# The first column blocks behind seven norms, computed from values that are not yet normalised

## The chip, the core and the metric

The kernel runs on one core of one Trainium2 chip. The core has TensorE (PE, matrix products), VectorE (DVE), ScalarE (ACT), GpSimd (POOL) and SyncE (SP, which issues nearly all DMAs). Each engine works through its own queue in order and waits on semaphores. The metric is device time in microseconds (us), the median of several runs.

## What is computed

A sequence of 256 positions with 1024 features passes through two blocks of two layers each, all in fp32 accuracy. With LN a LayerNorm and RMS an RMS norm:

```
x = LN(x; ln0)
for l in 0, 1:                                   # first block
    x = LN(a*x + mix(x @ w_in[l]) @ w_out[l]; ln1)      # attention, pooling, mLSTM
    u, g = split(x @ w_up[l])
    x = LN(a*x + (silu(conv3(g)) * u) @ w_down[l]; ln2)
for l in 0, 1:                                   # second block
    sh1, sc1, g1, sh2, sc2, g2 = split(silu(c) @ w_ada[l] + b_ada[l])
    h = RMS(x)*(1 + sc1) + sh1                   # rms0
    x = x + g1 * (conv and band attention of (h @ w_in2[l])) @ w_out2[l]
    h = RMS(x)*(1 + sc2) + sh2                   # rms1
    x = x + g2 * (dense SwiGLU (l = 0: ffn_gu, ffn_down) or 8 experts, top 2 (l = 1))(h)
```

## The kernel before

**Layout.** Activations stand transposed: 8 tiles of 128 features by 256 positions (`xT`, `hT`). Weights come in chunks of 1 MB (8 tiles of 128 rows by 256 columns: a column block) through a ring of four slots; SP issues a load when the slot's last reader is done.

**Split products.** For accuracy with fast products a weight is split: ACT copies a rounded high half (`whi`, L1027), DVE subtracts it for the low half (`wlo`, L1403). Activations are split likewise into `HH` (ACT, L1075) and `HL` (DVE, L1486). A product is then three matmuls (`mm3`), 48 for a column block (`pair`). There are buffers for two split chunks, so ACT and DVE work two chunks ahead (`two_ahead`, `ahead`), and the high half of chunk n+2 waits until PE has used chunk n.

**Norm.** `norm_tile` subtracts a pilot mean (DVE, L1436, LayerNorms only) and squares (ACT, L1051); in `norm_finish` PE sums over features with a matrix of ones, partial sums first and then the last two tiles. ACT and DVE make variance, root (L1060, L1063) and reciprocal (L1471), DVE centres (L1460) and multiplies (L1480), ACT applies weight and shift (L1070). While the statistics are made PE runs six filler products (`busy`, from constants). The first column block behind the norm is a `pair_whole`: the raw fp32 weights times `hT`, tile by tile as L1070 delivers them, 16 fp32 products of two records each. Meanwhile ACT makes all of `HH` and DVE then all of `HL` (`low_parts`). The second block is a `pair`. This goes for seven norms: ln0, ln1 (twice), ln2 of layer 0, rms0 (twice), rms1 of layer 0.

**Who uses the first block.** Behind ln0 and ln2 it is the query input `cq` (ACT L1079). Behind ln1 it is w_up's block 0: ACT taps it (L1237), DVE convolves (L1725), ACT applies SiLU (L1240; in layer 0 also to the row c, L1245), DVE gates (L1713) and makes the low part (`midl`, L1715). Behind rms0 ACT takes the sigmoid (L1274) and DVE the gate (L1809), then five taps of a convolution (L1782, L1786), then splits w_in2's third block. Behind rms1 it is ffn_gu's block 0.

**Modulation.** sh1 to g2 of both layers take 96 steps on DVE (`mod_step`, L1499), each with a 512 KB load into one of two buffers (SP, L1982). They are spread in three times 32: one behind each of w_up's blocks 1 to 21 of both layers and of ffn_gu's, and the other 11 between the chunks of w_down or ffn_down.

## Time and profile before

| | |
|---|---|
| median of 3 runs | 2084.1 us (2083.78 to 2084.38) |
| the profiled execution | 2083.09 us |
| its span, first to last instruction | 2081.1 us |
| busy: PE, DVE, ACT | 98%, 84%, 64% of the span |
| mean granted clock of PE | 0.995 |

Busy time of PE includes filler, and the ends of matmuls are modelled, so short waits between them are hidden in it. The experts of the last layer (from about 1066 us) are not touched by the change.

### The profile page before, as it was taken

The numbers are of one execution on the slowest core, as the hardware profiler recorded it, in microseconds if no ns is written. First come the engines' busy times: TensorE is split into PE (matmuls) and PEld (weight loads), VectorE is DVE, ScalarE is ACT, GpSimd is POOL, SyncE is SP. The second block draws the span as 40 slices with busy tenths as digits, with TensorE's granted clock in tenths as the row PEclk, the third lists the DMA queues.
The fourth block names the chain that finished last, engine by engine and source line by source line (L and its number), as shares of the span: only waits on it lengthen the run. The fifth ranks groups of instructions, "written<-read, shape, count | busy, mean of one in ns | idle before, by whom it ended". The sixth has DMA issues, their size and how long they took to land.

```text
span 2081.1 us, 31128 instructions
## 1 busy us (share of the span) xinstructions
PE 2038.9 (98%) x12718; PEld 1792.9 (86%) x12718; DVE 1754.4 (84%) x2299; ACT 1339.6 (64%) x1839; POOL 3.6 (0%) x23
## 2 busy tenths in 40 slices
PE   9999999999999999999989999999999999999998
PEld 8889999889998789998788888888888888888886
DVE  6779986789987967787869998888989889898987
ACT  4655545655545565445667777777777777777775
POOL 0000000000000000000000000000000000000000
PEclk9999999999999999999999999999999999999999
DMA  5358783348784438785449999999999999999994
GB/s 209 127 196 280 256 299 135 128 185 287 252 302 176 162 112 306 273 301 202 144 165 358 364 362 348 345 363 366 362 351 344 362 365 361 347 351 367 364 359 183
DMA packets 94179, 578.53 MB, mean 278 GB/s; under 512 B 11600, under 2 KB 14672, under 8 KB 35792
## 3 DMA queue, kind: packets, MB, share of 16 engines
q1 hardware_dynamic: 92592, 570.03, 74.0%
q10 hardware_dynamic: 1152, 3.32, 0.4%
q0 software_dynamic: 288, 3.15, 0.4%
q8 instruction: 102, 1.67, 0.3%
q14 instruction: 45, 0.37, 0.0%
HBM read 572.27 MB, written 1.05 MB: 275 GB/s over the span
## 4 chain that ended last, share of the span: by engine, by line
PE 76%; DVE 17%; ACT 5%; DMA 1%; issue 1%; SPq 0%; DVEq 0%; ACTq 0%
PE bank L2061 46%; PE bank L512 28%; DVE wlo L1403 6%; DVE side L1499 2%; DVE arena L1725 2%; DMA ring<-in_w_in 1%; PE bank L2119 1%; ACT arena L1240 1%; DVE RSTD L1471 1%; DVE midl L1715 1%; ACT whi L1027 1%; ACT midh L1229 1%; DVE XC L1480 0%; DVE XC L1460 0%; ACT HH L1082 0%
## 5 line engine op out<-in xcount | busy, mean ns | idle before, releaser
L1027 ACT ACTIVATE whi<-ring 128x1024 fp32r<-128x1024 f32 (+1 forms) x766 | 756.0, 1020 | 148.7 <-PE bank L512 66.1
L1403 DVE TENSOR_TENSOR wlo_moe<-ring,whi 128x1024 fp32r<-128x1024 f32 x448 | 526.4, 1220 | 9.6 <-ACT whi L1027 6.9
L512 PE MATMUL bank<-HH,whi 128*128 128x256 f32 x1536 | 430.6, 280 | 4.3 <-DVE wlo L1403 3.0
L512 PE MATMUL bank<-HL,whi 128*128 128x256 f32 x1536 | 424.3, 276 | 0.0
L512 PE MATMUL bank<-HH,wlo 128*128 128x256 f32 x1536 | 424.3, 276 | 0.0
L1403 DVE TENSOR_TENSOR wlo<-ring,whi 128x1024 fp32r<-128x1024 f32 (+3 forms) x318 | 343.6, 1114 | 76.4 <-ACT whi L1027 76.2
L512 PEld LDWEIGHTS bank<-HH,whi 128*128 128x128 f32 x1536 | 288.4, 188 | 8.7 <-DVE wlo L1403 4.2
L512 PEld LDWEIGHTS bank<-HL,whi 128*128 128x128 f32 x1536 | 288.5, 188 | 0.9 <-issue 0.5
L512 PEld LDWEIGHTS bank<-HH,wlo 128*128 128x128 f32 x1536 | 288.4, 188 | 0.0
L1403 DVE TENSOR_TENSOR extra_lo<-ring,extra_hi 128x1024 fp32r<-128x1024 f32 x224 | 264.4, 1221 | 14.7 <-ACT extra_hi L1027 14.4
L1027 ACT ACTIVATE extra_hi<-ring 128x1024 fp32r<-128x1024 f32 x224 | 229.8, 1061 | 41.1 <-PE bank L2061 41.1
L2061 PE MATMUL bank<-whi,xg 128*128 128x512 f32 x672 | 220.5, 396 | 0.0
L512 PE MATMUL bank<-midh,whi 128*128 128x256 f32 x528 | 148.3, 281 | 5.7 <-DVE midl L1715 3.3
L2061 PEld LDWEIGHTS bank<-whi,xg 128*128 128x128 f32 x672 | 126.3, 188 | 27.1
L512 PE MATMUL bank<-midl,whi 128*128 128x256 f32 x528 | 147.3, 279 | 0.0
L512 PE MATMUL bank<-midh,wlo 128*128 128x256 f32 x528 | 147.2, 279 | 0.0
L2061 PE MATMUL bank<-whi,xg_hh 128*128 128x512 f32 x336 | 134.7, 401 | 0.3 <-DVE wlo_moe L1403 0.3
L2061 PE MATMUL bank<-whi,xg_ht 128*128 128x512 f32 x336 | 131.6, 392 | 0.0
L2061 PE MATMUL bank<-wlo_moe,xg 128*128 128x512 f32 x336 | 131.6, 392 | 0.0
L2061 PE MATMUL bank<-wlo_moe,xg_hh 128*128 128x512 f32 x336 | 131.5, 391 | 0.0
L1499 DVE CUSTOM_DVE_ANT_0 side<-side,vec 128x1024 f32<-128x1024 f32 x96 | 122.8, 1279 | 0.5 <-DMA side<-in_w_ada 0.5
L512 PEld LDWEIGHTS bank<-midh,whi 128*128 128x128 f32 x528 | 100.7, 191 | 6.9 <-DVE midl L1715 3.7
(293 smaller groups left out, 3463.5 us busy)
## 6 DMA issues: line engine op xcount, KB each, us to landing
ring<-in_moe_gate SPq DMA_DIRECT2D x112, 1024.0 KB, 5.8
ring<-in_moe_up SPq DMA_DIRECT2D x112, 1024.0 KB, 6.7
ring<-in_moe_down SPq DMA_DIRECT2D x112, 1024.0 KB, 5.5
side<-in_w_ada SPq DMA_DIRECT2D x96, 512.0 KB, 4.3
ring<-in_w_up SPq DMA_DIRECT2D x44, 1024.0 KB, 4.9
ring<-in_w_in SPq DMA_DIRECT2D x32, 1024.0 KB, 5.5
ring<-in_w_down SPq DMA_DIRECT2D x32, 704.0 KB, 5.2
ring<-in_ffn_gu SPq DMA_DIRECT2D x22, 1024.0 KB, 4.8
```

Of the source, the lines that this page charges most:

```text
L512: return pe.matmul(out, lhsT, rhs, start=start, stop=stop, skip_group_check=True)
L1027: a.activation(hi, part, ACT.Copy).then_inc(*made.up(("hi", n, i)))
L1229: a.activation(MIDH[:, j, :], GC[j % 3], ACT.Copy).then_inc(*a_ffn.up(("mid", *key, j)))
L1240: a.activation(gc, gc, ACT.Silu).then_inc(*a_ffn.up(("silu", "w_down", l, j)))
L1403: v.tensor_tensor(lo, part, hi.bitcast(F32), ALU.subtract).then_inc(*done.up(("lo", n, i)))
L1471: v.reciprocal(RSTD[:, 0, :], RSTD[:, 0, :]).then_inc(*v_norm.up((s.name, "rstd")))
L1499: v.tensor_tensor_reduce(side_in[n % 2], side_in[n % 2], crow, 1.0, W(f"b_ada{l}", at), ALU.mult, ALU.add, modT[:, l, at:at + 1]).then_inc ...
L1715: v.tensor_tensor(MIDL[:, j, :], gc, MIDH[:, j, :].bitcast(F32), ALU.subtract).then_inc(*v_ffn.up(("mid", *key, j)))
L1725: v.scalar_tensor_tensor(gc[:, s:S], b[:, S:512 - s], W(f"w_fconv{l}", (2 - s) * NJ + j), gc[:, s:S], ALU.mult, ALU.add).then_inc(*v_ffn.u ...
L2061: return pe.matmul(out, lhsT, rhs, start=start, stop=stop, skip_group_check=True)
L2119: tm = pe.transpose(b[:, 128 * k:128 * k + 128], SGB[n % 2][:, 128 * k:128 * k + 128], ident)
```

## The change

Seven norms no longer have a filler and a `pair_whole`. While the tiles arrive, ACT makes a scaled copy of each, `ZT` (the tile times the norm's weight, not centred and not divided), with the weight (and for LayerNorms the shift) as extra columns. PE multiplies the first block's raw weights with `ZT` (`ahead_pair`): one of the eight pairs of products stands between the sums of the last tiles, three in rms0 of layer 0, none in ln0, the rest behind the sums. When the statistics are in, DVE scales the result, adds the product of mean and extra column (`ahead_made`), and the readers add the other extra column as a bias. `HH` and `HL` are now made in turn with the normalised tiles, and the second block takes them as they come (`pair_as_made`). Centring waits until the tile's copy in `ZT` is made. The 96 modulation steps are placed anew (`MOD_AT`): 24 in each layer of the first block (behind every second block of w_up, and 13 in w_down), 48 in the dense feed-forward (32 in ffn_gu, 16 in ffn_down); their loads follow six chunks behind the step two before (`mod_loads`).

The core of the diff; the reference to the same pattern in other stages is left out:

```diff
+        at_z = (2 * NJ + 3) * S
+        ZT = arena[:, at_z:at_z + 8 * (S + 2)].rearrange("p (k c) -> p k c", k=8)
+        AH, ends_ah = SQ[:, 6:8, :], small[:, 16:20]
...
+        AHEAD = {"ln0": ("w_in", 0, 1), ("ln2", 0): ("w_in", 1, 1), ("rms1", 0): ("ffn_gu", 0)}
+        for l in range(DEPTH):
+            AHEAD |= {("ln1", l): ("w_up", l, 0), ("rms0", l): ("w_in2", l, 0)}
+
+        MOD_AT = {}
+        for l in range(DEPTH):
+            MOD_AT |= {("w_up", l, j): 1 for j in range(1, NJ, 2)} | {("w_down", l, m, c): 1 for m in range(7) for c in range(2)}
+            del MOD_AT["w_down", l, 6, 1]
+        MOD_AT |= {("ffn_gu", j): 2 if j % 2 else 1 for j in range(1, NJ)}
+        MOD_AT |= {("ffn_down", m, c): 1 for m in range(8) for c in range(2)}
+        mod_slots = [CH[key] for key in sorted(MOD_AT, key=lambda key: CH[key]) for _ in range(MOD_AT[key])]
+        assert len(mod_slots) == 96, len(mod_slots)
+        mod_loads = {}
+        for n in range(2, 96):
+            mod_loads.setdefault(mod_slots[n - 2] + 6, []).append(n)
...
+            def ahead_pair(s):
+
+                key = AHEAD[s.name]
+                n = CH[key]
+                order = FIRST_ORDER if s.name == "ln0" else tuple(range(8))
+                cols_ = S + 2 if s.about else S + 1
+                banks = [take(*key, m, until=[(v_norm, s.name, "scaled", m)]) for m in range(2)]
+                w = raw_tile(n)
+                pe.wait_ge(*ARRIVED[n])
+                for k in order:
+                    pe.wait_ge(*a_norm(s.name, "z", k))
+                    for m in range(2):
+                        tm = mm(banks[m][:, 0:cols_], w[:, k, 128 * m:128 * m + 128], ZT[:, k, 0:cols_], k == order[0],
+                                k == order[-1])
+                    if k == order[-1]:
+                        tm.then_inc(*p_w.up(("raw", n), (*key, 0), (*key, 1)))
+                    yield
+
...
+                first = ahead_pair(s) if s.name in AHEAD else None
+                between = (1, 3, 5) if s.direct == 8 else (lim,) if s.direct == 2 else ()
...
                 for k in tiles:
...
+                    if first and k in between:
+                        next(first)
                 pause()
                 pause()
-                if end:
+                if first:
+                    for _ in first:
+                        pass
+                elif end:
                     busy(end, s.name)
...
+            def pair_as_made(key, src, until):
+
+                n = CH[key]
+                b = take(*key, until=until)
+                ws = [half(n, m) for m in range(2)]
+                for k in range(8):
+                    pe.wait_ge(*ready_h(src, k))
+                    for m in range(2):
+                        tm = mm3(b[:, S * m:S * m + S], [x[:, k, :] for x in ws[m]], H(k), k + m == 0, k == 7)
+                tm.then_inc(*p_w.up(("half", n, 0), ("half", n, 1), (*key, 0), (*key, 1)))
...
-                pair_whole(("w_in", l, 1), [(a_proj, "cqs0", l)])
-                pair(("w_in", l, 2), src, [(a_proj, "xp1", l)])
+                pair_as_made(("w_in", l, 2), src, [(a_proj, "xp1", l)])
...
+                    if j > 0:
+                        (pair_as_made if j == 1 else pair)(("w_up", l, j), ("ln1", l), [(v_ffn, "gated", "w_down", l, j)])
...
+                if s.name in AHEAD and s.name != "ln0":
+                    ahead_tile(s, k)
+
...
+            def ahead_tile(s, k):
+
+                gain, *_ = ends = ahead_columns(s)
+                if k == (FIRST_ORDER[0] if s.name == "ln0" else 0):
+                    for i, x in enumerate(ends if s.about else ends[1:]):
+                        a.activation(ZT[:, :, S + i], x, ACT.Copy).then_inc(*a_norm.up((s.name, "column", i)))
+                a.wait_ge(*(v_norm(s.name, "xc", k) if s.about else s.ready(k)))
+                a.activation(ZT[:, k, 0:S], (XC if s.about else s.src)[:, k, :], ACT.Copy, scale=gain[:, k:k + 1]).then_inc(
+                    *a_norm.up((s.name, "z", k)))
+
...
                     a.activation(RS[:, 0, :], PS[BANK[s.name, "mean"]][:, 0:S], ACT.Square, scale=1.0 / s.kt).then_inc(*a_norm.up((s.name, "mean2")))
+                    for k in beside:
+                        ahead_tile(s, k)
                     a.wait_ge(*v_norm(s.name, "var"))
...
-                if not then:
-                    for k in range(0, 8, 2):
-                        a.wait_ge(*a_norm(s.name, "dst", k + 1))
-                        a.activation(HH[:, k:k + 2, :], dst[:, k:k + 2, :], ACT.Copy).then_inc(
-                            *a_norm.up((s.name, "hh", k), (s.name, "hh", k + 1)))
+                    if behind:
+                        ahead_tile(behind, k)
+                    if not then and k % 2:
+                        a.wait_ge(*a_norm(s.name, "dst", k))
+                        a.activation(HH[:, k - 1:k + 1, :], dst[:, k - 1:k + 1, :], ACT.Copy).then_inc(
+                            *a_norm.up((s.name, "hh", k - 1), (s.name, "hh", k)))
...
-            norm_dev(N["ln0"])
+            for k in FIRST_ORDER[0:2]:
+                ahead_tile(N["ln0"], k)
+            norm_dev(N["ln0"], FIRST_ORDER[2:3])
+            for k in FIRST_ORDER[3:]:
+                ahead_tile(N["ln0"], k)
             split(CH["w_in", 0, 2], (0,))
             affine(N["ln0"], hT, lambda k: W("ln0_g", k), lambda k: W("ln0_b", k))
             split(CH["w_in", 0, 2], (1,))
...
                 split(CH["w_in", l, 3])
+                for m in range(2):
+                    a.wait_ge(*v_norm(IN[l], "ahead", m))
+                    a.activation(cq[:, m, :], AH[:, m, :], ACT.Identity, bias=ends_ah[:, 2 * m + 1:2 * m + 2]).then_inc(
+                        *a_proj.up(("cq0", l)))
+                    a.activation(SQ[:, m, :], AH[:, m, :], ACT.Square, bias=ends_ah[:, 2 * m + 1:2 * m + 2]).then_inc(
+                        *a_proj.up(("cqs0", l)))
...
+                    if j == 0:
+                        a.wait_ge(*v_norm(("ln1", l), "ahead", 1))
+                        a.activation(AH[:, 1, :], AH[:, 1, :], ACT.Identity, bias=ends_ah[:, 3:4]).then_inc(*a_ffn.up(("first", l)))
+                        a.wait_ge(*a_ffn("first", l))
+                        gate_in = AH[:, 1, :]
+                    else:
+                        a.wait_ge(*p_w("w_up", l, j, 1))
+                        gate_in = PS[BANK["w_up", l, j]][:, S:512]
+                    a.activation(gc, gate_in, ACT.Identity, bias=W(f"b_fconv{l}", j),
                                  scale=W(f"w_fconv{l}", 2 * NJ + j)).then_inc(*a_ffn.up(("tap", l, j)))
                     a.wait_ge(*v_ffn("conv", l, j))
...
+                    if c == 0:
+                        a.wait_ge(*v_norm(("rms0", l), "ahead", 1))
+                        a.activation(SG[:, 0, :], AH[:, 1, :], ACT.Sigmoid, bias=ends_ah[:, 3:4]).then_inc(*a_att.up(("sg", l, c)))
+                        return
...
+                    if j == 0:
+                        a.wait_ge(*v_norm(("rms1", 0), "ahead", 1))
+                        a.activation(GC[0], AH[:, 1, :], ACT.Silu, bias=ends_ah[:, 3:4]).then_inc(
...
                     v.wait_ge(*p_norm(s.name, "mean"))
+                    if s.name in AHEAD:
+                        for k in range(lo, hi):
+                            v.wait_ge(*a_norm(s.name, "z", k))
                     v.scalar_tensor_tensor(XC[:, lo:hi, :], bc(PS[BANK[s.name, "mean"]][:, 0:S], 2), -1.0 / s.kt, XC[:, lo:hi, :], ALU.mult,
...
+                    if s.name in AHEAD and j > 0:
+                        low_part(s, 2 * j - 2)
+                if s.name in AHEAD:
+                    low_part(s, 6)
+
+            def low_part(s, k):
+                v.wait_ge(*a_norm(s.name, "hh", k + 1))
+                v.tensor_tensor(HL[:, k:k + 2, :], hT[:, k:k + 2, :], HH[:, k:k + 2, :].bitcast(F32), ALU.subtract).then_inc(
+                    *v_norm.up((s.name, "hl", k), (s.name, "hl", k + 1)))
...
+            def ahead_made(s):
+
+                key = AHEAD[s.name]
+                if s.about:
+                    v.wait_ge(*v_norm(s.name, "rstd"))
+                    v.scalar_tensor_tensor(RS[:, 1, :], PS[BANK[s.name, "mean"]][:, 0:S], -1.0 / s.kt, RSTD[:, 0, :], ALU.mult,
+                                           ALU.mult).then_inc(*v_norm.up((s.name, "nmr")))
+                v.wait_ge(*p_w(*key, 1))
+                lo, n = (0, 2) if s.about else (1, 1)
+                for m in range(2):
+                    v.tensor_copy(ends_ah[:, 2 * m + lo:2 * m + 2], PS[BANK[(*key, m)]][:, S:S + n]).then_inc(
+                        *v_norm.up((s.name, "ends", m)))
+                for m in range(2):
+                    v.tensor_tensor(AH[:, m, :], PS[BANK[(*key, m)]][:, 0:S], RSTD[:, 0, :], ALU.mult).then_inc(
+                        *v_norm.up((s.name, "scaled", m), *([] if s.about else [(s.name, "ahead", m)])))
+                if s.about:
+                    for m in range(2):
+                        v.wait_ge(*v_norm(s.name, "scaled", m))
+                        v.scalar_tensor_tensor(AH[:, m, :], RS[:, 1, :], ends_ah[:, 2 * m:2 * m + 1], AH[:, m, :], ALU.mult,
+                                               ALU.add).then_inc(*v_norm.up((s.name, "ahead", m)))
...
+            def mod_beside(*key):
+                for _ in range(MOD_AT.get(key, 0)):
+                    mod_step(next(mod_steps))
...
             norm_finish(N["ln0"])
-            split(CH["w_in", 0, 2], (0,))
-            low_parts(N["ln0"])
-            split(CH["w_in", 0, 2], (1,))
+            split(CH["w_in", 0, 2])

             for l in range(DEPTH):
                 split(CH["w_in", l, 3])
+                ahead_made(N[IN[l]])
...
                     two_ahead(CH["w_up", l, j])
-                    gc, b = GC[j % 3], PS[BANK["w_up", l, j]]
+                    gc = GC[j % 3]
+                    if j == 0:
+                        ahead_made(N["ln1", l])
+                    gate_in = AH[:, 1, :] if j == 0 else PS[BANK["w_up", l, j]][:, S:512]
                     v.wait_ge(*a_ffn("tap", l, j))
...
-                    if j > 0:
-                        mod_step(l, j - 1)
+                    mod_beside("w_up", l, j)
...
                 def gate(c):
                     ahead(CH["w_in2", l, c])
-                    v.wait_ge(*a_att("sg", l, c))
-                    v.tensor_tensor(Z[:, c, :], PS[BANK["w_in2", l, c]][:, 0:S], SG[:, c % 2, :], ALU.mult).then_inc(
-                        *v_att.up(("z", l, c)))
+                    if c == 0:
+                        ahead_made(N["rms0", l])
+                        v.wait_ge(*a_att("sg", l, c))
+                        v.scalar_tensor_tensor(Z[:, c, :], AH[:, 0, :], ends_ah[:, 1:2], SG[:, 0, :], ALU.add, ALU.mult).then_inc(
+                            *v_att.up(("z", l, c)))
...
+                modulated_gain(1, l)
...
-                rms_modulated(1, l)
+                norm_finish(N["rms1", l])
...
+                    if j == 0:
+                        ahead_made(N["rms1", 0])
                     if j > 0:
                         gated(("ffn_down",), ("ffn_gu", j - 1), j - 1)
-                    if j > 0:
-                        mod_step(2, j - 1)
+                    mod_beside("ffn_gu", j)
...
+                g.wait_ge(*p_w("raw", CH["w_in", l, 1]))
...
+                g.wait_ge(*p_w("raw", CH["w_in2", l, 0]))
...
+            def mod_load(n):
+                if n >= 2:
+                    sp.wait_ge(*v_mod("step", n - 2))
+                sp.dma_start(side_in[n % 2], t["w_ada"][n // 48, n // 8 % 6, n % 8]).then_inc(s_side[n % 2], 16)
...
-                    next(mod)
+                    mod_load(0)
+                    mod_load(1)
...
+                for k in mod_loads.get(n, ()):
+                    mod_load(k)
```

## Rows read from the trace of the kernel before

**Rows 1.** The page, busy time by engine, and shares of the chain that ended last.
```profile
PE 2038.9 (98%) x12718; PEld 1792.9 (86%) x12718; DVE 1754.4 (84%) x2299; ACT 1339.6 (64%) x1839; POOL 3.6 (0%) x23
...
PE 76%; DVE 17%; ACT 5%; DMA 1%; issue 1%; SPq 0%; DVEq 0%; ACTq 0%
```

**Rows 2.** Windows (stretch, length, busy by engine with count, granted clock, DMA share, GB/s).
```profile
160.00:245.00 85.00, 85.00 (x753) 85.00 (x752) 77.20 (x122) 47.05 (x76) 0.00 (x0) 1.00 0.82 277
247.00:280.40 33.40, 30.37 (x243) 29.59 (x242) 29.18 (x49) 15.28 (x26) 0.00 (x0) 0.95 0.76 254
270.22:273.63 3.41, 3.41 (x19) 3.41 (x18) 3.41 (x6) 0.53 (x2) 0.00 (x0) 0.50 0.59 207
...
569.00:592.00 23.00, 20.37 (x159) 19.71 (x158) 19.73 (x33) 9.63 (x16) 0.00 (x0) 0.93 0.78 267
...
785.00:885.00 100.00, 100.00 (x884) 100.00 (x884) 79.08 (x111) 49.54 (x75) 0.00 (x0) 1.00 0.78 283
```

**Rows 3.** Timeline of PE, two waits (start, length, instruction, idle time before and releaser).
```profile
268.34 0.38 PE L512 MATMUL bank<-midh,whi 128*128 128x256 f32 x1 [1.61 <-DVE midl L1715]
...
749.89 0.38 PE L512 MATMUL bank<-HH,whi 128*128 128x256 f32 x1 [1.10 <-DVE wlo L1403]
```

**Rows 4.** Timeline of DVE, one round in w_up of layer 0.
```profile
199.57 1.28 DVE L1499 CUSTOM_DVE_ANT_0 side<-side,vec 128x1024 f32<-128x1024 f32 x1
...
203.04 0.99 DVE L1725 SCALAR_TENSOR_TENSOR arena<-bank,vec,arena 128x255 f32<-128x255 f32 x2
...
205.19 1.28 DVE L1499 CUSTOM_DVE_ANT_0 side<-side,vec 128x1024 f32<-128x1024 f32 x1
```

**Rows 5.** Timeline of PE behind the sums: ln0, ln1, rms0 of layer 0.
```profile
18.76 7.14 PE L512 MATMUL bank<-hT,ring 128*128 128x256 f32 x32 [2.30 <-ACT hT L1070]
...
132.51 2.75 PE L512 MATMUL bank<-cst 128*128 128x256 f32 x12
136.74 7.14 PE L512 MATMUL bank<-hT,ring 128*128 128x256 f32 x32 [1.48 <-ACT hT L1070]
...
646.25 3.69 PE L512 MATMUL bank<-SQ,cst 128*128 128x256 f32 x16 [0.33 <-DVE SQ L1439]
```

**Rows 6.** DMA issues: the modulation's loads (count, size, us to landing).
```profile
side<-in_w_ada SPq DMA_DIRECT2D x96, 512.0 KB, 4.3
```

**Rows 7.** Timeline of ACT behind ln1 of layer 0.
```profile
136.00 1.09 ACT L1070 ACTIVATE hT<-XC,vec 128x256 f32<-128x256 f32 x2 [2.28 <-DVE XC L1480]
...
141.32 2.17 ACT L1075 ACTIVATE HH<-hT 128x512 fp32r<-128x512 f32 x4
...
148.10 1.04 ACT L1245 ACTIVATE side<-side 128x1024 f32<-128x1024 f32 x1
```

**Rows 8.** Timeline of ACT, squares and splits in w_out and w_out2.
```profile
113.67 0.75 ACT L1051 ACTIVATE SQ<-XC 128x256 f32<-128x256 f32 x2 [3.09 <-DVE XC L1436]
114.32 1.99 ACT L1027 ACTIVATE whi<-ring 128x1024 fp32r<-128x1024 f32 x2
...
746.62 0.94 ACT L1051 ACTIVATE SQ<-xT 128x256 f32<-128x256 f32 x2 [3.10 <-DVE xT L1763]
```

**Rows 9.** Timeline of DVE behind ln1 of layer 0.
```profile
133.75 1.75 DVE L1471 RECIPROCAL RSTD<-RSTD 128x256 f32<-128x256 f32 x1
...
136.93 0.69 DVE L1480 TENSOR_TENSOR XC<-XC,RSTD 128x512 f32<-128x512 f32 x1
...
141.96 2.50 DVE L1486 TENSOR_TENSOR HL<-hT,HH 128x512 fp32r<-128x512 f32 x4 [1.68 <-ACT HH L1075]
```

**Rows 10.** Timeline of DVE behind ln0.
```profile
14.97 1.75 DVE L1471 RECIPROCAL RSTD<-RSTD 128x256 f32<-128x256 f32 x1
...
25.68 1.23 DVE L1403 TENSOR_TENSOR wlo<-ring,whi 128x1024 fp32r<-128x1024 f32 x1
```

**Rows 11.** Timeline of DVE behind rms0 of layer 0.
```profile
661.14 0.42 DVE L1809 TENSOR_TENSOR arena<-bank,RS 128x256 f32<-128x256 f32 x1 [0.96 <-ACT RS L1274]
...
664.01 2.35 DVE L1403 TENSOR_TENSOR wlo<-ring,whi 128x1024 fp32r<-128x1024 f32 x2
```

More of the change, by code:

```diff
@@ L840, in pe_program @@
                 for j in range(NJ):
-                    if j == 0:
-                        pair_whole(("w_up", l, 0), [(v_ffn, "gated", "w_down", l, 0)])
-                    else:
-                        pair(("w_up", l, j), ("ln1", l), [(v_ffn, "gated", "w_down", l, j)])
+                    if j > 0:
+                        (pair_as_made if j == 1 else pair)(("w_up", l, j), ("ln1", l), [(v_ffn, "gated", "w_down", l, j)])
                 for m in range(8):
@@ L1064, in norm_dev, with affine @@
                         *a_norm.up((s.name, "dev")))
-            def affine(s, dst, gain, bias, then=False):
+            def affine(s, dst, gain, bias, then=False, behind=None):
                 a.wait_ge(s_vec, 16)
@@ L1255, in act_program @@
                 else:
-                    affine(N["ln2", 1], xT, lambda k: W("ln2_g1", k), lambda k: W("ln2_b1", k), then=True)
+                    affine(N["ln2", 1], xT, lambda k: W("ln2_g1", k), lambda k: W("ln2_b1", k), then=True, behind=N["rms0", 0])
             def rms_modulated(which, l):
@@ L1501, in mod_step, with modulated_gain @@
                     *v_mod.up(("step", n), *([("mod", l, i)] if k == 7 else [])))
+            def mod_beside(*key):
+                for _ in range(MOD_AT.get(key, 0)):
+                    mod_step(next(mod_steps))
+            def modulated_gain(which, l):
+                sc = 8 if which == 0 else 32
+                v.wait_ge(*v_mod("mod", l, 1 if which == 0 else 4))
+                v.wait_ge(s_vec, 16)
+                v.scalar_tensor_tensor(amod[:, which, :], modT[:, l, sc:sc + 8], 1.0,
+                                       W("nmix%d" % l if which == 0 else "nffn%d" % l, 0, 8), ALU.add, ALU.mult).then_inc(
+                    *v_norm.up(((("rms0", "rms1")[which], l), "amod")))
             def low_of_mix(k, src, name):
@@ L1766, in dve_program @@
             for l in range(DEPTH):
[L1767 removed]
+                norm_finish(N["rms0", l])
+                v.wait_ge(*p_w("raw", CH["w_in2", l, 0]))
                 v.reduce_sum(rows32, ident.rearrange("p (r j) -> p j r", r=4), AX_X).then_inc(*v_tap.up(("rows32", l)))
@@ L2028, in sp_program @@
                         delayed_rows(l, 3)
-                for _ in range(steps_behind(chunks[n - NSLOT][0]) if NSLOT <= n < first_moe else 0):
-                    next(mod)
+                for k in mod_loads.get(n, ()):
+                    mod_load(k)
         def in_use(used):
```

114 lines of the change are left out of this document (39 added, 75 removed).

## The prediction

> **What bounds the kernel now.** I read the page first, then the stretches by engine (windows), then the timelines around each norm. The page shows TensorE (PE) busy almost all the time, and the chain that ended last runs through PE for three quarters of the span and through VectorE (DVE) for most of the rest [rows 1]. So only time that PE loses in waits, or spends on filler, can be won. The windows show two kinds of stage [rows 2]. In a steady feed-forward stretch PE starts 753 matmuls in 85 us, 0.113 us each: a split column block (48 matmuls) takes 5.44 us and no wait is seen. At the two passages from w_up to w_down, 243 matmuls take 33.4 us where 27.5 would do, and 159 take 23.0 where 18.0 would do; about 0.2 us of each difference is the pilot product. The waits there are for DVE [rows 3]. The reason is in DVE's own round: one modulation step of 1.2 us, two low parts, convolution and gating, and the next step starts 5.62 us after this one [rows 4]. That is 0.18 us per column block more than PE's 5.44, so DVE falls back until PE has nothing to do.
>
> The second loss is the norm itself. After the sums of ln1 PE runs 12 filler records (2.75 us), idles 1.48 us and computes the first column block from fp32 values, 32 records in 7.14 us, 0.44 us for each of 16 products [rows 5]. The second block starts at 143.5 and ends at 149.0, 16.5 us after the fillers began.
>
> **What the change removes: the fall-back of DVE.** In w_up every second block keeps its modulation step. DVE's round becomes 5.62 - 1.2/2 = 5.02 us on average against PE's 5.44. The waits at both passages go: 5.9 - 0.2 = 5.7 and 5.0 - 0.2 = 4.8, together **-10.5 us**. The steps that leave go mostly to the dense feed-forward stage, where DVE is busy 79 of 100 us and half a step more per block (0.6 us of 5.44) fits [rows 2]. Each moved step takes its 512 KB load along: SyncE waits for step n-2 before it issues load n, and the next weight load stands behind that wait. A step's load lands in 4.3 us [rows 6] and the weights are fetched four chunks ahead, so I cost it at nothing; without that cover, one late load would stall DVE by at most those 4.3 us. GpSimd's fills now wait for the early block instead of the last low part, which is sooner: nothing.
>
> **What it adds at a norm.** Eight scaled tiles (z) on ScalarE (ACT); no row shows a Copy with a column scale, so I bound it: 0.33 us (spacing of the plain squares) and 0.50 (spacing of the affine tiles, which have scale and bias) [rows 7, 8]; I take 0.43, nearer the second because it too reads a column. On DVE, for a LayerNorm: one product of mean and deviation, two tiny copies, two scalings, two additions; from 0.34 to 0.42 us each and 0.1 for a copy, about 2.05 us; for an RMS norm 1.1 us. On ACT one extra pass before the first tap, 0.55 us as an affine tile. The extra columns add 2 of 256 to 16 products, under 0.1 us.
>
> **ln1, step by step (twice).** DVE's chain after the sums: reciprocal to 135.5, tiles 2 and 3 normalised from 136.93 [rows 9]. With a low part (2.50/4 = 0.63) behind each pair, a pair costs 0.71 + 0.61 + 0.63 = 1.94 us. ACT keeps up: two affine tiles 1.09 and one copy 0.54 are 1.66 with the waits between [rows 7]. The last low part ends at about 144.3, the second block, made as the low parts come, at 144.3 + 12 x 0.113 = 145.7 instead of 149.0. That is 3.3 us gained, if the third and fourth blocks are there.
>
> They are not. The wait for the scaled block stands in ACT's queue ahead of the split of w_up 3. DVE: two low parts of w_up 2 to 147.0, the new pieces to 149.0. ACT: added pass and tap to 150.1. DVE: convolution 0.99 [rows 4] to 151.2. ACT: SiLU 0.42, in layer 0 also the row c (0.95 [rows 7]), then the high half 1.04; DVE its low half 1.22: ready at 155.0 in layer 0 and 154.1 in layer 1. PE wants it at 145.7 + 5.44 = 151.1 and waits 3.9 and 3.0 us. Before, it started there at 143.5 + 5.5 + 5.44 = 154.5. So the 3.3 us are lost again, with 0.5 on top in layer 0 and -0.4 in layer 1; DVE then delivers w_up 4 another 0.4 late.
>
> And the sums come later. The split of w_out 2 starts on ACT right behind the squares of tiles 0 and 1 [rows 8]; now two columns (0.2) and two z stand before it, +1.1 us, and two more z before the next split, +0.45. DVE's residuals follow these splits, so the last tile is 1.6 us late. Sum: +0.5 + 0.4 + 1.6 = **+2.5 us** in layer 0, -0.4 + 0.4 + 1.6 = **+1.6** in layer 1.
>
> **ln0.** The centring of tiles 0 and 1 now waits for their z. These are the second and third ACT jobs behind the square root, so the reciprocal that began at 14.97 begins 1.9 us later, at 16.9. From reciprocal to last low part takes 144.3 - 133.75 = 10.6 us as in ln1: 27.5. Only then come both low halves of the second block (2.36): 29.8, and PE wants both before its first product. Before, it began at 18.76 + 6.9 = 25.6 and the second half, ready at 26.9, was in time [rows 5, 10]. **+4.2 us**; PE idles some 8 us in it, as its early block is over by 22.
>
> **ln2 of layer 0.** Same chain: -3.3, the sums 0.8 later (one pair of products stands among them), and the split of chunk 4 stands on ACT behind four copies of the scaled block, about +1.4: **-1.1 us**.
>
> **rms0 (twice).** Here the wait has a short path. The third block's low part follows the first gate and five taps on DVE: gate at 661.14, low part at 664.01, done 1.22 later [rows 11]; sums had ended at 649.9 [rows 5], so it began 14.1 behind them. Now the gate waits for the new pieces: last low part at 10.3, 1.1 for the pieces, 0.5 for the sigmoid, gate and taps 2.9, so low part from 15.0 to 16.3. The second block is over at 11.8; PE idles 4.5 us, then starts the third block 0.4 us later than before (15.9). In layer 0, three pairs of products (0.86 each) stand among the sixteen records of the sums [rows 5], where 0.33 us were idle: +2.4: **+2.8 us**. In layer 1 two modulation steps now lie on DVE in the last row of ffn_down, before the last residual: about +1.0, **+1.4 us**.
>
> **rms1 of layer 0.** The only clean one: no convolution between block and split. Second block over at 11.8 instead of 15.9 behind the sums; w_up 3's counterpart is ready at 16.7, wanted at 17.3. -4.1. But the split of w_out2 2, for which PE waits already (1.10 us [rows 3]), stands behind two squares [rows 8] and now also two z: +0.9. **-3.2 us**.
>
> **Clock.** With the fillers gone, the long waits matter for PE's clock. In the trace a wait of 1.61 us to 268.3 [rows 3], with shorter ones beside it, went ahead of a fall: from 270.2 the granted clock was 0.50, the 1.2 GHz level, for 3.4 us with 19 matmuls where 30 fit: 11 x 0.113 = 1.2 us lost, up to 1.7 if all of it is used [rows 2]. The 1.48 us idle behind ln1's fillers left the clock at full. The new waits are 8, 3.9, 3.0, 4.5 and 4.5 us; I take five falls at 1.06 us after what they hide: **+5.3 us**. Bounds: none, and 1.7 for each of six (w_out2's wait too), 10.2.
>
> The Trainium skill (TensorE: Matmul & The Clock Gate, "HAM oscillation — how this bites in real kernels") says that waits between bursts of matmuls let the clock fall to half, again at every such wait. By that rule all of the new waits are paid in full and the sum is that of the third rival below; the trace agrees as far as it goes, with its fall at 270.2.
>
> **Sum.** -10.5 + 2.5 + 1.6 + 4.2 - 1.1 + 2.8 + 1.4 - 3.2 = -2.3; with the clock +3.0. The profiled execution took 2083.1 us (span 2081.1); the median of the runs, 2084.1, lies 1.0 above, so I predict **2087.1 us**: no difference to speak of. Within 0.2% (4.2 us) a measurement of this kernel does not tell a change from none.
>
> **Rivals.** (1) The waits behind the norms go for good, because the work between block and third split is shorter than I add up: -10.5 - 3.3 x 3 - 4.1 x 3 = -33 at most, 2051 us. For it speaks that PE's filler and idle time is real [rows 5]; against it the order of ACT's and DVE's programs, which is fixed. Chance 0.06. (2) The same waits, but the clock holds and z costs 0.33: -2.3 - 2.5 = -5, 2079 us, just faster. For it: the waits of 1.5 us that cost no clock. Chance 0.14. (3) Slower: each new wait is followed by a full fall, -2.3 + 10.2 = +7.9, 2092 us. It decides from 6.5 us of falls on. For it: the fall behind a wait of 1.61 us. Chance 0.33. (4) The moved steps do not free w_up, as DVE, starting each w_up late, never catches up: +3.0 + 10.5, 2098 us. Against it: 0.42 us per block over 17 blocks. Chance 0.05. My forecast, a draw within 0.2%, has 0.42.
>
> **Range.** From just past rival 2 to past rival 3: 2077 to 2096; the likeliest case alone, 2080 to 2088. Faster 0.20, same 0.42, slower 0.38.
>
> **What the next profile would show.** No PE wait for a low part of w_down or of midl at the two passages; modulation steps two apart in w_up. PE idle before the fourth w_up block, released by the low part, 3 to 4 us; before the third w_in2 block about 4.5 us; before the second block of ln0 about 8 us, followed by stretches at 0.50. Scaled tiles of 0.33 to 0.50 us on ACT. If PE goes from the fourth block on without a wait, the ACT queue is not what I think, and I am wrong to the fast side; if waits at the passages remain, to the slow side.

## The result and the profile after

The changed kernel took 2114.8 us (median of 4, 2112.2 to 2116.8) against 2083.9 before: a ratio of 1.0146, 95% interval 1.0131 to 1.0161. That is 31 us slower, where 3 were forecast and at most 12 allowed for. The profiled execution took 2114.85 us (span 2111.4).

Three lines of the page after: PE's and DVE's busy time, the chain that ended last by engine, and the group of the modulation steps (busy, mean ns, then DVE's idle time ahead of them and what ended it).

```profile
PE 2039.8 (97%) x12634; PEld 1788.3 (85%) x12634; DVE 1766.3 (84%) x2339; ACT 1362.9 (65%) x1912; POOL 3.5 (0%) x23
...
PE 59%; DVE 24%; ACT 9%; DMA 6%; issue 2%; DVEq 0%; SPq 0%; ACTq 0%
...
L1608 DVE CUSTOM_DVE_ANT_0 side<-side,vec 128x1024 f32<-128x1024 f32 x96 | 122.7, 1281 | 17.1 <-DMA side<-in_w_ada 16.4
```

The last of these in the kernel before:

```profile
L1499 DVE CUSTOM_DVE_ANT_0 side<-side,vec 128x1024 f32<-128x1024 f32 x96 | 122.8, 1279 | 0.5 <-DMA side<-in_w_ada 0.5
```

Against [rows 1], PE's share of the chain falls from 76 to 59% and the shares of DVE, ACT and DMA grow: the work that ended last now runs through PE's suppliers. DMA, at 1% before, has 6, and the third line says which loads DVE waits for: it stood still 16.4 us for those of modulation steps. Before, that was 0.5 us.

Windows of the changed kernel (columns as in [rows 2]): behind ln0, the two passages, and two stretches of the dense feed-forward stage.

```profile
24.40:34.30 9.90, 4.73 (x22) 4.76 (x23) 8.04 (x14) 5.70 (x10) 0.00 (x0) 0.50 0.38 122
266.30:282.50 16.20, 15.50 (x135) 15.30 (x134) 13.78 (x23) 8.14 (x13) 0.00 (x0) 1.00 0.67 233
576.20:592.40 16.20, 15.55 (x135) 15.34 (x134) 13.78 (x23) 8.16 (x15) 0.00 (x0) 1.00 0.67 230
800.00:900.00 100.00, 94.84 (x813) 93.07 (x812) 82.41 (x119) 43.40 (x68) 0.00 (x0) 1.00 0.86 300
903.00:968.00 65.00, 61.09 (x516) 59.18 (x515) 52.16 (x81) 26.70 (x47) 0.00 (x0) 1.00 0.91 318
```

The passages are nearly cleared: 135 matmuls in 16.2 us, at full clock. One large loss is in the fourth row: 813 matmuls in 100 us where the kernel before had 884 [rows 2], 71 x 0.113 = 8 us lost in this stretch alone, in a stage in which nothing was lost before.

PE's long waits in the changed kernel, from its timeline (last in brackets: the idle time and what ended it).

```profile
29.57 0.55 PE L530 MATMUL bank<-HH,whi 128*128 128x256 f32 x1 [8.86 <-DVE wlo L1486]
...
162.58 0.36 PE L530 MATMUL bank<-HH,whi 128*128 128x256 f32 x1 [3.40 <-DVE wlo L1486]
...
472.54 0.36 PE L530 MATMUL bank<-HH,whi 128*128 128x256 f32 x1 [2.47 <-DVE wlo L1486]
...
671.69 0.39 PE L530 MATMUL bank<-HH,whi 128*128 128x256 f32 x1 [4.11 <-DVE wlo L1486]
...
758.36 0.58 PE L530 MATMUL bank<-HH,whi 128*128 128x256 f32 x1 [2.14 <-DVE wlo L1486]
...
912.15 0.39 PE L530 MATMUL bank<-midh,whi 128*128 128x256 f32 x1 [2.07 <-DVE midl L1839]
...
976.55 0.80 PE L530 MATMUL bank<-SQ,cst 128*128 128x256 f32 x1 [5.78 <-ACT SQ L1088]
...
994.03 0.55 PE L530 MATMUL bank<-HH,whi 128*128 128x256 f32 x1 [3.51 <-DVE wlo L1486]
```

Six are the waits of the prediction in their places: ln0, fourth block behind each ln1, third block behind each rms0, third block of w_out2. Two were not foreseen: 2.07 us at the passage from ffn_gu to ffn_down, for the same low part as at w_up's passages before, and 5.78 us ahead of the last sums of rms0 of layer 1.

To see where the 31 us lie, I read the same instruction in several timelines: the start of the first or last product of a stage. First column: the kernel before, us; then how much later each of three kernels is there (the two single parts are experiments, below).

| start of | before | changed | steps alone | early blocks alone |
|---|---|---|---|---|
| second block behind ln0 | 25.55 | +4.0 | +1.6 | +4.0 |
| w_out, layer 0 | 112.75 | +6.2 | +1.7 | +6.2 |
| last of w_up, layer 0 | 258.22 | +8.0 | +1.3 | +11.1 |
| last of w_down, layer 0 | 324.10 | +6.9 | -1.5 | +12.3 |
| w_out, layer 1 | 424.75 | +5.1 | -0.9 | +10.8 |
| last of w_up, layer 1 | 569.90 | +6.2 | -0.9 | +15.1 |
| last of w_down, layer 1 | 635.28 | +3.1 | -4.3 | +14.6 |
| last of w_in2's first blocks, layer 0 | 698.81 | +7.5 | -4.3 | +18.9 |
| last of w_out2, layer 0 | 760.83 | +10.0 | -4.4 | +19.6 |
| last of ffn_gu | 887.96 | +14.1 | +0.9 | +16.0 |
| last of ffn_down | 947.80 | +20.9 | +6.0 | +16.9 |
| second block behind rms0, layer 1 | 960.19 | +24.5 | +12.2 | +12.7 |
| last of w_in2's first blocks, layer 1 | 998.66 | +29.8 | +12.2 | +19.3 |

The +1.6 of the steps alone in the first row is not theirs, as nothing is changed there. Behind the same wait of 2.30 us the whole products of ln0 took 7.14 us at full clock in the kernel before [rows 5], but in this execution 8.83, with a stretch at the half clock:

```profile
18.70 8.83 PE L533 MATMUL bank<-hT,ring 128*128 128x256 f32 x32 [2.30 <-ACT hT L1154]
```

```profile
19.10:22.50 3.40, 3.40 (x10) 2.69 (x9) 3.33 (x5) 3.05 (x7) 0.00 (x0) 0.50 0.54 222
```

So a difference of 1.6 us between two single profiles is no sign of the change there.

### The profile page after: what moved, and what is told of

It reads as the page before. It is cut to its first block, busy times and chain, and to the rows that moved or that the text cites. A ratio compares the mean times of both kernels' runs of the same rounds, so it can differ in the third digit from the quotient of the medians.

```text
span 2111.4 us, 31090 instructions
## 1 busy us (share of the span) xinstructions
PE 2039.8 (97%) x12634; PEld 1788.3 (85%) x12634; DVE 1766.3 (84%) x2339; ACT 1362.9 (65%) x1912; POOL 3.5 (0%) x23
## 4 chain that ended last, share of the span: by engine, by line
PE 59%; DVE 24%; ACT 9%; DMA 6%; issue 2%; DVEq 0%; SPq 0%; ACTq 0%
PE bank L2173 45%; PE bank L530 12%; DVE wlo L1486 10%; DMA side<-in_w_ada 5%; DVE side L1608 4%; ACT whi L1064 3%; DVE arena L1852 2%; PE bank L2231 1%; ACT hT L1131 1%; DVE RSTD L1557 1%; ACT arena L1314 1%; DVE midl L1839 1%; DVE XC L1566 1%; DVE XC L1546 1%; ACT HH L1137 0%
## 5 line engine op out<-in xcount | busy, mean ns | idle before, releaser
L530 PE MATMUL bank<-HH,whi 128*128 128x256 f32 x1536 | 437.1, 285 | 37.1 <-DVE wlo L1486 32.6
L1608 DVE CUSTOM_DVE_ANT_0 side<-side,vec 128x1024 f32<-128x1024 f32 x96 | 122.7, 1281 | 17.1 <-DMA side<-in_w_ada 16.4
```

Of the source, the lines that this page charges most:

```text
L530: return pe.matmul(out, lhsT, rhs, start=start, stop=stop, skip_group_check=True)
L1608: v.tensor_tensor_reduce(side_in[n % 2], side_in[n % 2], crow, 1.0, W(f"b_ada{l}", at), ALU.mult, ALU.add, modT[:, l, at:at + 1]).then_inc ...
```

## The experiments

**First four: the two halves of the change.**

Steps alone (`mod_alone`): no early blocks, so all seven norms keep filler and whole products. The line that empties the list, in the changed kernel; the rest of the edit, left out here, brings back what a norm outside the list needs.

```diff
+        SEVEN = set(AHEAD)
+        AHEAD = {k: x for k, x in AHEAD.items() if k in ()}
```

> The kernel before with the new places of the modulation steps and of their loads alone; the seven norms keep filler and whole products. Theory A (the moved steps come back as waits for their loads: between the start of the dense feed-forward stage and the second block behind rms0 of layer 1 the changed kernel lost 24.5 - 5.3 = 19.2 us against the kernel before): the two passages give some 8.6 us, the dense stage takes some 19, so 2083.9 - 8.6 + 19.2 = about 2094 us. Theory B (the prediction's: moved steps cost nothing, the loss of 31 us is made at the norms): 2083.9 - 10.5 = about 2073 us.

Measured: 2096.6 us, ratio 1.0057 (1.0040 to 1.0073). The moved steps alone cost 11.6 us against the 2085.0 of the kernel before beside them; A holds, B falls. DVE's idle time until a step's load landed (us, times), from the view of the steps' tile:

```profile
  DMA side<-in_w_ada: 18.8, 23
```

Early blocks alone (`ahead_alone`): a step behind every block again, loads as before.

```diff
-            MOD_AT |= {("w_up", l, j): 1 for j in range(1, NJ, 2)} | {("w_down", l, m, c): 1 for m in range(7) for c in range(2)}
+            MOD_AT |= {("w_up", l, j): 1 for j in range(1, NJ)} | {("w_down", l, m, c): 1 for m in range(6) for c in range(2)}
...
-        MOD_AT |= {("ffn_gu", j): 2 if j % 2 else 1 for j in range(1, NJ)}
+        MOD_AT |= {("ffn_gu", j): 1 for j in range(1, NJ)}
...
-            mod_loads.setdefault(mod_slots[n - 2] + 6, []).append(n)
+            mod_loads.setdefault(mod_slots[n - 2] + 5, []).append(n)
```

> The changed kernel with the modulation steps where they were (a step behind every block of w_up and ffn_gu, 32 in each third), so only the early first blocks remain of the change. Theory A: 2114.8 - 10.6 = about 2104 us, no waits for modulation loads in the dense stage, the waits at the two passages from w_up to w_down back. Theory B: 2114.8 + 10.5 = about 2125 us.

Measured: 2103.2 us, 1.0089 (1.0072 to 1.0105), 18.2 us above before, as A has it. The two halves add up: 11.6 + 18.2 = 29.8, of the 31 measured together.

Loads sooner (`loads_sooner`): of the diff above only the last pair of lines, in the changed kernel.

> The changed kernel with one number changed: the load of step n is issued behind the fifth weight chunk after the block of step n - 2 and not behind the sixth. Theory A1 (the loads are late because SyncE issues them a block too late): most of the 19 us in the dense stage come back, about 2100 us. Theory A2 (with two buffers and three steps in two blocks the landing time itself, 5.9 us in that stage, is too long whatever the place of the issue): under 6 us come back, 2109 to 2115 us. Theory B (loads play no part): 2114.8 us.

Measured: 2108.5 us, 1.0114 (1.0095 to 1.0133): 6.4 us come back, just past what A2 allows and far from A1: the place of the issue is worth at most a third of the 19 us. The same line of the steps' tile for the changed kernel:

```profile
  DMA side<-in_w_ada: 16.4, 19
```

And for this kernel; two thirds of it stay:

```profile
  DMA side<-in_w_ada: 10.8, 11
```

Why it stays is seen in the changed kernel's dense stage, first in DVE's timeline, then in SyncE's.

```profile
845.99 1.28 DVE L1608 CUSTOM_DVE_ANT_0 side<-side,vec 128x1024 f32<-128x1024 f32 x1 [0.82 <-DMA side<-in_w_ada]
...
850.71 1.28 DVE L1608 CUSTOM_DVE_ANT_0 side<-side,vec 128x1024 f32<-128x1024 f32 x1
...
852.26 1.29 DVE L1608 CUSTOM_DVE_ANT_0 side<-side,vec 128x1024 f32<-128x1024 f32 x1 [0.26 <-DMA side<-in_w_ada]
...
858.48 1.28 DVE L1608 CUSTOM_DVE_ANT_0 side<-side,vec 128x1024 f32<-128x1024 f32 x1 [1.41 <-DMA side<-in_w_ada]
```

```profile
847.31 0.33 SPq L2106 DMA_DIRECT2D side<-in_w_ada  x1
849.58 0.33 SPq L2130 DMA_DIRECT2D ring<-in_ffn_gu  x1
852.03 0.33 SPq L2106 DMA_DIRECT2D side<-in_w_ada  x1
```

The step at 858.48 uses the buffer of the step at 850.71, two before it, which ends at 851.99. SyncE issues the load at 852.03, at once; it lands 6.4 us later, 7.7 after that step's start. In a rhythm of two steps in one block and one in the next, the three steps come due some 5.4, 9.7 and 6.6 us after the start of the one two before them (5.44 for a block, 1.2 for a step). Two of three are late, though the issue waits for nothing but the buffer. The chain that ended last, in the changed kernel from 790 to 860 us, goes from step to load to step; its shares by line there:

```profile
by line: DMA side<-in_w_ada 43.1%; DVE side L1608 22.9%; DVE wlo L1486 22.7%; ACT midh L1441 4.3%; DVE midl L1839 4.3%; DVE arena L1837 2.9%; issue 0.7%; DVE arena L1834 0.6%; DVE modT L1608 0.2%
```

Steps spread (`spread_alone`): as steps alone, but a step behind three of four blocks of w_up and one behind each block of the dense stage; loads five chunks behind, as in loads sooner.

```diff
+            MOD_AT |= {("w_up", l, j): 1 for j in range(1, NJ) if j % 4} | {("w_down", l, m, c): 1 for m in range(7) for c in range(2)}
...
+        MOD_AT |= {("ffn_gu", j): 1 for j in range(1, NJ)}
         MOD_AT |= {("ffn_down", m, c): 1 for m in range(8) for c in range(2)}
+        MOD_AT["ffn_gu", 11] = 2
```

> The kernel before with other places for the modulation steps: three of four blocks in w_up, 13 of 16 in w_down, one behind each block of the dense stage (one block has two); loads behind the fifth chunk. Theory A: the passages from w_up to w_down go as in the changed kernel and nothing comes back, 2083.9 - 8.6 = about 2075 us; DVE's round in w_up is then 5.62 - 1.2/4 = 5.32 us against PE's 5.44. If only the halving of the steps frees w_up, the passages keep part of their waits, 2079 us or more.

Measured: 2081.8 us, 0.9986 (0.9976 to 0.9995): 3.2 us won, not 9. ffn_gu runs without loss, but here too PE waits ahead of the last sums of rms0 of layer 1, as in its timeline:

```profile
947.70 0.80 PE L534 MATMUL bank<-SQ,cst 128*128 128x256 f32 x1 [5.57 <-ACT SQ L1112]
```

Between the last product of ffn_down and the second block behind rms0, 12.4 us before, lie 18.4 us. The steps in the last two rows of ffn_down wait for their loads and stand ahead of the last residual.

**Second four: places that cost nothing, and the order of the splits.**

Steps spread, last rows clear (`spread_clear`); this is the base of all later runs but one.

```diff
+            MOD_AT |= {("w_up", l, j): 1 for j in range(1, NJ) if j % 5} | {("w_down", l, m, c): 1 for m in range(7) for c in range(2)}
...
+        MOD_AT |= {("ffn_gu", j): 2 if j in (6, 11, 16) else 1 for j in range(1, NJ)}
+        MOD_AT |= {("ffn_down", m, c): 1 for m in range(6) for c in range(2)}
```

> The kernel before with the modulation steps spread once more: four of five blocks in w_up, 13 of 16 in w_down, one behind each block of ffn_gu (three blocks have two), and none in the last two rows of ffn_down, where the run with all 16 filled lost 6.0 us to late loads ahead of the last residual and half a clock window behind it. Theory: steps cost time only where their load comes late ahead of work that PE waits for, so this gains the passages (some 8 us) and loses about 1 us at each of the three double steps: about 2079 us against 2084 to 2085. If the last rows were not the cause, it stays at spread_alone's time, 2082 us.

Measured: 2077.4 us, 0.9962 (0.9949 to 0.9976), 7.7 us below before. The same line of the steps' tile, and the window of ffn_gu:

```profile
  DMA side<-in_w_ada: 0.2, 1
```

```profile
767.00:881.20 114.20, 114.20 (x1009) 114.17 (x1008) 92.00 (x129) 56.62 (x84) 0.00 (x0) 1.00 0.79 293
```

DVE waits for loads no more, and PE starts 1009 products in 114.2 us, 0.113 each. The moved steps pay when each load has time.

Two early blocks (`clean_two`): on this base, early first blocks behind ln2 of layer 0 and rms1 of layer 0 only.

```diff
+        AHEAD = {k: x for k, x in AHEAD.items() if k in (('ln2', 0), ('rms1', 0))}
```

> The last kernel with the early first block at two norms alone, ln2 of layer 0 and rms1 of layer 0. Theory (order of the queues: these two have no convolution or gate between the early block and the third block's split): 1.0 + 2.9 = 3.9 us below spread_clear, about 2075 us. Rival (any early block costs, as it takes the filler away and lets the clock fall): no better than spread_clear, 2079 us or more.

Measured: 2075.2 us, 0.9952 (0.9938 to 0.9965), 2.2 us below `spread_clear` where 3.9 were expected. So an early block can pay, but something takes a part.

Splits sooner (`splits_sooner`): in the changed kernel. The first part below is ACT's, the second DVE's (which leaves out j == 1 as well), the third is in the gate of both.

```diff
-                    two_ahead(CH["w_up", l, j])
+                    if j != 1:
+                        two_ahead(CH["w_up", l, j])
+                    if j == 0:
+                        two_ahead(CH["w_up", l, 1])
...
                         ahead_made(N["ln1", l])
+                        two_ahead(CH["w_up", l, 1])
...
-                    ahead(CH["w_in2", l, c])
+                    if c != 2:
+                        ahead(CH["w_in2", l, c if c == 3 else c + 1])
```

> The changed kernel with the splits of the next blocks moved ahead of the early block's own work: behind ln1 the split of w_up 3 stands ahead of ACT's wait for the scaled block and ahead of the convolution on DVE; behind rms0 the splits of the third and fourth blocks stand ahead of the gate. Theory (PE waits 3.7, 2.8, 4.4 and 3.8 us behind these four norms because the low part stands behind the block's own work): some 2 us come back at each ln1 and 3 to 5 at each rms0, 10 to 14 in all, 2101 to 2105 us. Rival (the waits only move on to the next block): 2112 to 2115 us.

Measured: 2110.1 us, 1.0117 (1.0102 to 1.0133): 4.7 us come back, not 10 to 14. The waits of 3.40 us at 162.58 and 4.11 at 671.69 are gone, but:

```profile
166.54 0.36 PE L530 MATMUL bank<-HH,whi 128*128 128x256 f32 x1 [1.64 <-DVE wlo L1490]
...
679.92 0.67 PE L530 MATMUL bank<-whi,HH 128*128 128x512 f32 x1 [1.99 <-DVE wlo L1490]
```

The waits are shorter and one block further on: the rival holds for more than half of what was hoped for.

All that was thought good (`six_sooner`): steps as in `spread_clear`, six early blocks (not ln0), splits sooner.

> The steps placed as in spread_clear, the early first block at six norms (ln0 keeps filler and whole products), and the splits sooner. If both theories hold, with 2 us less at each ln1 and 2 at each rms0 than without early blocks: about 2079 - 3.9 - 8 = 2067 us. If the clock's falls decide, 2079 us or more.

Measured: 2089.5 us, 1.0021 (1.0012 to 1.0031), 12 us above `spread_clear`. My theory of the order of the splits falls as a remedy: what DVE owes behind ln1 comes due later, at the passage to w_down, where four steps in five blocks leave it 5.62 - 1.2/5 = 5.38 us a round against PE's 5.44, no room to catch up:

```profile
270.48 0.39 PE L533 MATMUL bank<-midh,whi 128*128 128x256 f32 x1 [1.65 <-DVE midl L1888]
```

**Last four: single norms.**

Scaled tiles later (`clean_two_late`): as `clean_two`, but ACT makes each scaled tile behind the next splits (the False tells `norm_tile` to leave it out).

```diff
+                    if ("ln2", l) in AHEAD:
+                        for k in (0, 1) if m == 2 else (m - 1,) if m > 2 else ():
+                            ahead_tile(N["ln2", l], k)
                     for k in () if m == 0 else (0, 1) if m == 1 else (m,):
-                        norm_tile(N["ln2", l], k)
+                        norm_tile(N["ln2", l], k, False)
...
+                    if ("rms1", l) in AHEAD and c > 0:
+                        for k in (2 * c - 2, 2 * c - 1):
+                            ahead_tile(N["rms1", l], k)
                     for k in (2 * c, 2 * c + 1):
-                        norm_tile(N["rms1", l], k)
+                        norm_tile(N["rms1", l], k, c == 3)
```

> The kernel with steps spread and early blocks behind ln2 of layer 0 and rms1 of layer 0, with each scaled tile moved on ACT behind the next splits of w_down and of w_out2 instead of ahead of them. Theory (the scaled tiles delay the splits: 0.5 us in each of four rows of w_down, together 2.0 us; 0.9 us and a fall of the clock at the third block of w_out2, together 2.3): 2075.2 - 4.3 = about 2071 us. Rival (the tiles are not what delays them, or moved they delay the sums): 2075 us or more.

Measured: 2071.0 us, 0.9931 (0.9918 to 0.9945): as expected, and 13.5 us below the kernel before. In ACT's timeline of `clean_two` the scaled tile (L1132) stands ahead of the split (L1087):

```profile
739.63 0.49 ACT L1132 ACTIVATE arena<-xT,amod 128x256 f32<-128x256 f32 x1
740.03 1.99 ACT L1087 ACTIVATE whi<-ring 128x1024 fp32r<-128x1024 f32 x2
```

In `clean_two_late` the split follows the squares at once:

```profile
738.00 0.94 ACT L1111 ACTIVATE SQ<-xT 128x256 f32<-128x256 f32 x2 [3.05 <-DVE xT L1930]
738.84 1.99 ACT L1087 ACTIVATE whi<-ring 128x1024 fp32r<-128x1024 f32 x2
...
740.84 0.89 ACT L1132 ACTIVATE arena<-xT,amod 128x256 f32<-128x256 f32 x2
```

PE's wait for that block goes from 1.79 us in `clean_two`, with a stretch at the half clock behind it, to 1.11 in `clean_two_late`, at full clock, as before (1.10, [rows 3]):

```profile
742.46 0.38 PE L533 MATMUL bank<-HH,whi 128*128 128x256 f32 x1 [1.79 <-DVE wlo L1520]
```

```profile
741.27 0.39 PE L533 MATMUL bank<-HH,whi 128*128 128x256 f32 x1 [1.11 <-DVE wlo L1528]
```

The 396 products of w_down take 45.0 us again (47.0 in `clean_two`).

ln0 alone, and ln0 with the wait filled (`ln0_alone`, `ln0_filled`), on the base of `spread_clear`:

```diff
                 src = IN[l]
+                if src == "ln0":
+                    busy(18, "wait")
```

> The steps spread as in spread_clear (2077.4 us) and the early first block behind ln0 alone. From the changed kernel's trace: the second block starts 4.0 us later, and 10 us at the half clock follow the wait of 9.2 us; 2077.4 + 4.0 to 6.3 = 2081 to 2084 us. The prediction's term was +4.2 without the clock.

> The last kernel with 18 filler products (about 0.46 us each, 8.3 us) on TensorE in the wait behind the early block of ln0. If the half clock behind that wait costs time of its own, about 2 us come back against ln0_alone (second block at +4.0, nothing lost behind it); if it lies in time that is lost anyway, the time is that of ln0_alone.

Measured: 2081.7 us (median of 11, 2079.9 to 2086.1) and 2080.7 (11, 2077.7 to 2082.0), each against 2084.5 before: 0.9988 (0.9979 to 0.9997) and 0.9978 (0.9969 to 0.9987). So an early block at ln0 costs 4.3 us against `spread_clear` (5.0 if each is set against the kernel before beside it), and filler gives about 1 of them back, though the ranges overlap. Windows of `ln0_alone`, then of `ln0_filled`:

```profile
24.20:34.20 10.00, 4.66 (x22) 4.69 (x23) 8.21 (x14) 5.81 (x10) 0.00 (x0) 0.50 0.39 130
```

```profile
29.50:40.30 10.80, 10.80 (x95) 10.80 (x96) 6.43 (x11) 4.54 (x9) 0.00 (x0) 1.00 0.30 103
```

The second blocks start at 29.54 and 29.48 us. With the wait filled the clock stays full, and the last product of the two blocks starts at 40.35 instead of 42.69. In these two profiles the half clock cost 2.3 us there; the medians show less, and why is not shown.

Convolution and gates (`four_gated`): on the same base, early blocks behind the two ln1 and the two rms0.

> The steps spread as in spread_clear and early first blocks behind the two ln1 and the two rms0 alone, whose first block goes on through a convolution or a gate. Stage by stage from the traces so far: +2.4 and +2.1 us for ln1 (from the start of w_out to the end of w_down), +4.4 and +3.3 for rms0, so 2077.4 + 12 = about 2089 us. By the prediction's terms without the clock +2.5 + 1.6 + 2.8 + 0.4 = 7.3, 2085 us. If early blocks are worth their filler, below 2077 us.

Measured: 2094.5 us, 1.0048 (1.0034 to 1.0062): 17.1 us above `spread_clear`, 5 more than the sum of stages read from the changed kernel. That kernel has a step behind every second block of w_up, and DVE makes good there what ln1 owes; here the waits at the passages are back:

```profile
270.48 0.38 PE L533 MATMUL bank<-midh,whi 128*128 128x256 f32 x1 [1.60 <-DVE midl L1884]
...
582.26 0.38 PE L533 MATMUL bank<-midh,whi 128*128 128x256 f32 x1 [1.61 <-DVE midl L1884]
```

## Why the prediction was wrong

**The step that failed** is the cost of the moved steps' loads: "I cost it at nothing; without that cover, one late load would stall DVE by at most those 4.3 us." Not one load was late but 19, DVE waited 16.4 us for them, and the median landing over all steps was 5.3 us instead of the 4.3 in [rows 6]. The prediction looked at DVE's busy time, into which half a step more fits (DVE is busy 82 of 100 us), and at the weights, which are four chunks ahead. It did not set the path of one buffer against the block: step, issue, landing, next step in the same buffer. From its own rows that path is 1.2 + 4.3 = 5.5 us at least, against the 5.44 that the new rhythm leaves to one step in three. By these numbers such a step would be hardly late; what made it dear is the landing. The 4.3 us are a median over stages: in ffn_down it was 5.8 already in the kernel before (10 loads), and in ffn_gu it went from 3.9 (21 loads) to 5.1 in the changed kernel (29 loads), 6.4 in the case above. In the steps-alone run ffn_gu loses 5.2 us, ffn_down 5.1, and the way to rms0 6.2, where "about +1.0" stood for the last row; the residual that the sums wait for stands behind two waiting steps. The 13 steps in w_down gave away another 2.3 and 1.3 us. In `spread_clear`, with one step behind each block of ffn_gu (three have two), none in the last two rows of ffn_down, the same 13 in w_down, and loads one chunk sooner, all of this is gone, with nothing changed but the places of steps and loads.

**The passages** were right: the first 132 products of w_down took 20.4 and 19.9 us before and 15.2 in both layers with the steps alone, -9.9 for a forecast of -10.5. For the steps as a whole the forecast was -10.5 + 1.0 (last row of ffn_down) = -9.5; measured alone they cost +11.6. That is off by 21, three quarters of the whole error of 28.

**The early blocks** cost 18.2 us alone; the terms said 12.5 with the clock's falls (7.2 and 5.3). Term by term:

- ln0: +4.2 forecast, the second block +4.0, and +6.2 behind the half clock. This is against an execution before whose whole products ran at full clock; against `spread_clear`, whose whole products did not, it is +2.4 and +4.6. So the +4.2 came true in part by luck of the execution.
- ln1: +2.5 and +1.6 forecast; +1.7 and +1.1 in the changed kernel from w_out's first product to w_up's last, with a step behind every second block; +3.1 and +2.5 behind four of five (`four_gated`), +4.9 and +4.3 behind every block (early blocks alone). The forecast waits of 3.9 and 3.0 us were 3.40 and 2.47. The queue's order on ACT was right; that the delay is kept or made good by the steps' density was missing.
- ln2: -1.1 forecast, -1.8 behind the sums, but the scaled tiles in w_down ate 2.0, as `clean_two_late` shows. At ln2 the sum had no term for the tiles; each stands on ACT ahead of a split of w_down, and four rows pay some 0.5 us each.
- rms0: +2.8 and +0.4 (without the moved steps) forecast, +4.4 in the changed kernel, +2.4 with early blocks alone in layer 1. The waits were 4.11 and 3.51 us for a forecast of 4.5. The +2.4 for the three pairs in layer 0 is 3 x 0.86 - 0.33 = 2.25 by its own numbers.
- rms1: -3.2 forecast, -3.7 in `clean_two_late`, -1.8 with the tiles ahead of the splits (`clean_two`).

**The clock**: five falls of 3.4 us were taken. Ahead of the last layer's experts the changed kernel has half-clock stretches behind ln0, both rms0, w_out2 and the late sums (24.3, 672.9, 758.2, 973.2 and 993.7 us), and none behind the waits of 3.40 and 2.47 us at ln1. The number of five came out, but not where it was put, and the stretch behind ln0 fills the whole 9.9 us of its window above. The Trainium skill (TensorE: Matmul & The Clock Gate, "HAM oscillation — how this bites in real kernels") tells of a kernel whose clock falls again at every wait for a load between bursts of matmuls, waits of some 3 to 5 us. The 3.40 us at ln1 of layer 0 are a wait of that length, and here the clock held; in `loads_sooner` the same wait was followed by a stretch at 0.50:

```profile
161.54 0.36 PE L530 MATMUL bank<-HH,whi 128*128 128x256 f32 x1 [3.41 <-DVE wlo L1486]
```

```profile
162.20:165.60 3.40, 3.40 (x18) 3.40 (x17) 2.88 (x6) 2.12 (x4) 0.00 (x0) 0.50 0.00 0
```

So neither the third rival's "each new wait" nor a count of waits gives the falls of one execution.

Of the rivals, the third (slower through the clock) went the right way, but its reason is not the main one. The fourth came near in kind, moved steps that do not free DVE, but not in place: w_up's passages were freed, and DVE fell back in the stage that the steps were moved to.

## What to carry to other kernels

Work that is moved takes its loads along, and a load has a path of its own: buffer free, issue, landing, use. Set that path against the shortest time that the new rhythm leaves between two uses of a buffer, with the landing time of the stage it moves into: here up to 7.7 us against 5.44. An average hides it: with the median landing of ffn_gu, 1.3 + 5.1 = 6.4 us, the path fits into the mean of the three times above, 7.2, but not into the shortest. And a stage whose engine is busy four fifths of the time can still have no room. Work made early paid here at two of seven norms, ln2 and rms1, where the next split does not stand behind the early block's own work. At ln0 it made the second block itself late, and at the other four moving the splits ahead of that work did not make it pay (`six_sooner`). Last, put added work behind what the bounding engine waits for, even when it is short: half a microsecond ahead of the splits of four rows cost the whole gain at one norm.

## What the runs showed of the hardware that I had not expected

The landing time of a 512 KB load is not one number: in the kernel before its median was 3.9 us in ffn_gu and 5.8 in ffn_down, and in ffn_gu of the changed kernel 5.1, while all loads together moved 296 GB/s there (290 before). And TensorE's clock did not fall behind every wait: 3.40 us without a product were passed over at ln1, while 2.14 us in w_out2 were followed by a stretch at 0.50. The length of the wait alone does not decide it, as the pairs of 2.30 and of 3.40 and 3.41 us above went both ways; what does stays open here.
